# DeltaNet mixer: triangular inversion over all four TensorE quarters, with the second direction half a level behind

## What is computed

```python
a_mat = jnp.where(strict, jnp.einsum('bhnik,bhnjk->bhnij', kb, k) * decay, 0.0)
rhs = jnp.concatenate([v * beta[..., None], kb * jnp.exp(gc)[..., None]], axis=-1)
sol = lax.linalg.triangular_solve(a_mat + jnp.eye(CHUNK, dtype=jnp.float32), rhs,
                                  left_side=True, lower=True, unit_diagonal=True)
```

```python
m = jnp.einsum('nd,de->ne', cond, w_ada_l.astype(jnp.float32)) + b_ada_l.astype(jnp.float32)
```

## Time and profile before

| | |
|---|---|
| median of 3 runs | 2075.03 us (2072.61 to 2078.57) |
| profiled execution, its own time | 2079.55 us |
| its span, first to last instruction | 2077.8 us |
| granted TensorE clock, mean | 0.929 |
| PE, PEld busy | 85%, 70% of the span |
| DVE, ACT, POOL busy | 62%, 46%, 10% |
| T, XX, YY products in the span | 5120 records on line 1100, with x0 |

### The profile page before, as it was taken

One profiled execution on the slowest core, in us unless ns is written; L12 is line 12 of the kernel. 1 busy time (PEld: TensorE's weight loads), 2 busy tenths in 40 slices (PEclk: granted clock), 3 DMA queues, 4 the chain that ended last, 5 costly groups with the idle time before them and its releaser, 6 DMA issues. The chain is left out here.

```text
span 2077.8 us, 40338 instructions
## 1 busy us (share of the span) xinstructions
PE 1763.5 (85%) x15365; PEld 1455.0 (70%) x15366; DVE 1296.8 (62%) x1885; ACT 961.8 (46%) x1490; POOL 209.0 (10%) x267
## 2 busy tenths in 40 slices
PE   3998879899696799999919988899986939999992
PEld 0898678788454588888818986788873527888882
DVE  2388255556445696896663883556662368999674
ACT  2244523233312786786432454333332138888651
POOL 0000022222000100000020001212220010000001
PEclk7999999999797899999959999999997969999996
DMA  7221093420313798897643111331004059999854
GB/s 313 71 82 44 31 358 126 154 102 2 107 59 152 285 384 340 335 401 286 228 153 98 55 44 51 127 125 52 3 2 145 31 209 385 397 398 397 355 199 165
DMA packets 112110, 376.64 MB, mean 181 GB/s; under 512 B 14730, under 2 KB 35490, under 8 KB 86374
## 3 DMA queue, kind: packets, MB, share of 16 engines
q1 hardware_dynamic: 83310, 303.85, 39.2%
q10 hardware_dynamic: 20168, 39.89, 5.0%
q0 software_dynamic: 8496, 30.94, 4.0%
HBM read 332.87 MB, written 41.78 MB: 180 GB/s over the span
## 5 line engine op out<-in xcount | busy, mean ns | idle before, releaser
L1955 DVE TENSOR_TENSOR expert_w_lo<-shared,expert_w_hi 128x2048 fp32r<-128x2048 f32 x192 | 430.6, 2285 | 44.6 <-ACT expert_w_hi L1897 44.3
L1897 ACT ACTIVATE expert_w_hi<-shared 128x2048 fp32r<-128x2048 f32 x192 | 360.6, 1915 | 42.4 <-PEq L141 37.8
L1839 PE MATMUL ps<-expert_w_hi,expert_x_hi 128*128 128x512 f32 x592 | 232.3, 392 | 5.1 <-DVE expert_x_lo L1951 5.1
L1840 PE MATMUL ps<-expert_w_lo,expert_x_hi 128*128 128x512 f32 x592 | 232.0, 392 | 0.0
L1841 PE MATMUL ps<-expert_w_hi,expert_x_lo 128*128 128x512 f32 x592 | 232.0, 392 | 0.0
L1839 PEld LDWEIGHTS ps<-expert_w_hi,expert_x_hi 128*128 128x128 f32 x592 | 112.2, 190 | 29.3 <-issue 5.9
L1841 PEld LDWEIGHTS ps<-expert_w_hi,expert_x_lo 128*128 128x128 f32 x592 | 112.1, 189 | 23.5
L1840 PEld LDWEIGHTS ps<-expert_w_lo,expert_x_hi 128*128 128x128 f32 x592 | 112.1, 189 | 23.2
L1875 PE MATMUL ps<-expert_w_hi,expert_hid_hi 128*128 128x512 f32 x296 | 118.5, 400 | 2.2 <-ACT expert_hid_hi L1929 1.2
L1011 POOL TENSOR_TENSOR mixer_NTb<-mixer_Bt,consts_sb 128x256 f32<-128x256 f32 x120 | 88.4, 760 | 286.3 <-DVE mixer_Bt L1286 222.7
L1876 PE MATMUL ps<-expert_w_lo,expert_hid_hi 128*128 128x512 f32 x296 | 115.4, 390 | 0.0
(11 more groups left out here) (344 smaller groups left out, 3741.1 us busy)
## 6 DMA issues: line engine op xcount, KB each, us to landing
shared<-in_w_gate SPq DMA_DIRECT2D x64, 1024.0 KB, 7.1
shared<-in_w_up SPq DMA_DIRECT2D x64, 1024.0 KB, 8.7
shared<-in_w_down SPq DMA_DIRECT2D x64, 1024.0 KB, 9.0
qkv<-in_w_ada SPq DMA_DIRECT2D x20, 1280.0 KB, 6.0
shared<-in_w_in SPq DMA_DIRECT2D x10, 2048.0 KB, 7.8
y_table<-expert_y ACTq DMA_DIRECT2D x37, 512.0 KB, 8.8
qkvT<-in_w_ada SPq DMA_DIRECT2D x20, 768.0 KB, 8.4
y_table<-zero ACTq DMA_DIRECT2D x1, 12800.0 KB, 50.9
```

What stands on the lines that cost most here:

```text
L1839: pe.matmul(bank, hi, w_hi[:, j, w], start=first, stop=False)
L1840: pe.matmul(bank, hi, w_lo[:, j, w], start=False, stop=False)
L1897: act.activation(w_hi[:, j, :], raw[:, j, :], ACT.Copy).then_inc(w_hi_done, 1)
L1955: dve.tensor_tensor(w_lo[:, j, :], raw[:, j, :], w_hi[:, j, :].bitcast(F32), ALU.subtract).then_inc(w_lo_done, 1)
```

## The change

Direction 1 keeps Y and T1 in the other half of the partitions (`place`), so that its T and XX products use the upper right and lower left quarters of the array, while direction 0 keeps the diagonal ones. Direction 1 lags by half a level: TensorE interleaves T of direction 0 with XX of direction 1 of the level before, product by product, then makes YY of direction 1; then it interleaves XX of direction 0 with T of direction 1, then makes YY of direction 0. YY stays in the diagonal quarters in both directions. `turn(n0)` and `next_scores(n0 + 1)` now stand between these two halves of level 2 and of level 3. x0 of both directions is interleaved too and waits for both Y. VectorE's first Y is written in two halves, since the halves change place. The order of the other instructions on VectorE, ScalarE, GpSimd and SyncE is as it was; the modulation units are as they were.

```diff
+        def place(d, b):
+
+            return b if d == 0 else 1 - b
...
-                def eight(b, c, lhsT, rhs, sem):
-
-                    for h in range(DH):
-                        for r in range(2):
-                            mm = pe.matmul(G.ps[half(r), b, 256 * c + h * HB:256 * c + (h + 1) * HB],
-                                           lhsT(h)[half(r)], rhs(h)[half(r)], start=True, stop=True)
-                    mm.then_inc(s_[sem], 1)
+                def x0(d, h, b):
+                    y = half(place(d, b))
+                    return pe.matmul(G.ps[half(b), d, h * HB:(h + 1) * HB], Y[y, d, h, :], G.c("eye")[y], start=True, stop=True)
+
+                def t1(v, d, h, b):
+                    return pe.matmul(G.ps[half(place(d, b)), d, h * HB:(h + 1) * HB], NTb[half(b), v % 2, d, h, :], X[half(b), d, h, :],
+                                     start=True, stop=True)
+
+                def xx(d, h, b):
+                    y = half(place(d, b))
+                    return pe.matmul(G.ps[half(b), d, 256 + h * HB:256 + (h + 1) * HB], Y[y, d, h, :], T1[y, d, h, :],
+                                     start=True, stop=True)
+
+                def yy(d, h, b):
+                    y = half(place(d, b))
+                    return pe.matmul(G.ps[y, 2 + d, h * HB:(h + 1) * HB], T1[y, d, h, :], Y[y, d, h, :], start=True, stop=True)
+
+                def wait_t1(s, v, d):
+                    pe.wait_ge(s_["nt_done"], lev(s, v, d))
+                    if v == 0:
+                        pe.wait_ge(s_["x0_done"], at(s, d))
+                    else:
+                        pe.wait_ge(s_["x_done"], lev(s, v - 1, d))
+
+                def wait_xx(s, v, d):
+                    pe.wait_ge(s_["t1_done"], lev(s, v, d))
+                    if v:
+                        pe.wait_ge(s_["y_done"], lev(s, v - 1, d, LV - 1))
+                    else:
+                        pe.wait_ge(s_["qk_done"], at(s, d))
+
+                places = [(h, b) for h in range(DH) for b in range(2)]
...
-                    for d in range(2):
-                        pe.wait_ge(s_["y0_done"], at(s, d))
-                        eight(d, 0, lambda h: Y[:, d, h, :], lambda h: G.c("eye"), "x0_p")
-                    for v in range(LV):
-                        for d in range(2):
...
-                            eight(d, 0, lambda h: NTb[:, v % 2, d, h, :], lambda h: X[:, d, h, :], "t1_p")
+                    pe.wait_ge(s_["y0_done"], at(s, 1))
+                    for h, b in places:
+                        m0 = x0(0, h, b)
+                        m1 = x0(1, h, b)
+                    m0.then_inc(s_["x0_p"], 1)
+                    m1.then_inc(s_["x0_p"], 1)
+                    for v in range(LV + 1):
+                        if v == 0:
+                            wait_t1(s, v, 0)
+                            for h, b in places:
+                                m0 = t1(v, 0, h, b)
+                            m0.then_inc(s_["t1_p"], 1)
+                        elif v < LV:
+                            wait_t1(s, v, 0)
+                            wait_xx(s, v - 1, 1)
+                            for h, b in places:
+                                m0 = t1(v, 0, h, b)
+                                m1 = xx(1, h, b)
+                            m0.then_inc(s_["t1_p"], 1)
+                            m1.then_inc(s_["xx_p"], 1)
+                        else:
+                            wait_xx(s, v - 1, 1)
+                            for h, b in places:
+                                m1 = xx(1, h, b)
+                            m1.then_inc(s_["xx_p"], 1)
+                        if v:
+                            for h, b in places:
+                                m1 = yy(1, h, b)
+                            m1.then_inc(s_["yy_p"], 1)
                         if v == 2:
                             turn(n0)
                         if v == 3:
                             next_scores(n0 + 1)
-                        for d in range(2):
-                            pe.wait_ge(s_["t1_done"], lev(s, v, d))
...
-                            eight(d, 1, lambda h: Y[:, d, h, :], lambda h: T1[:, d, h, :], "xx_p")
-                            eight(2 + d, 0, lambda h: T1[:, d, h, :], lambda h: Y[:, d, h, :], "yy_p")
+                        if v < LV:
+                            wait_xx(s, v, 0)
+                            wait_t1(s, v, 1)
+                            for h, b in places:
+                                m0 = xx(0, h, b)
+                                m1 = t1(v, 1, h, b)
+                            m0.then_inc(s_["xx_p"], 1)
+                            m1.then_inc(s_["t1_p"], 1)
+                            for h, b in places:
+                                m0 = yy(0, h, b)
+                            m0.then_inc(s_["yy_p"], 1)
...
-                        dve.tensor_tensor(Y[:, d], NTb[:, 1, d], row(G.c("eye"), DH), ALU.add).then_inc(s_["y0_done"], 1)
+                        for b in range(2):
+                            ins = dve.tensor_tensor(Y[half(place(d, b)), d], NTb[half(b), 1, d], row(G.c("eye")[half(b)], DH), ALU.add)
+                        ins.then_inc(s_["y0_done"], 1)
...
-                                    ins = dve.tensor_tensor(YF[half(b), d, :, half(b)], Y[half(b), d], blocks(2 + d)[half(b)],
-                                                            ALU.subtract)
+                                    y = half(place(d, b))
+                                    ins = dve.tensor_tensor(YF[half(b), d, :, half(b)], Y[y, d], blocks(2 + d)[y], ALU.subtract)
```

## The result

The changed kernel takes 2081.34 us (median of 20 runs, 2076.69 to 2085.85) against 2075.57 of the kernel before beside it: a ratio of 1.0027, interval 1.0016 to 1.0037. It is slower by 5.8 us where I had forecast 20 us less; the sign was wrong, by a difference of the size that I had called too small to tell.

What follows compares the result with a forecast made beforehand. Bounds per block: TensorE in levels 0 to 3, the division at level 2, VectorE at the end. Order net of Y0 14.5 plus clock 5.3 gave 19.8 us off 2079.55 profiled, so a 2055 us median; range 2047 to 2069.

Steps and rivals of the forecast that it cites:

- order and quarters: Mixer blocks: the new product order and shared quarters were to gain 15.9 us, before Y0's cost of 1.4.
- Y0: VectorE's first Y in four half adds instead of two: 1.4 us more, paid in each layer's first block, elsewhere hidden.
- Four quarters: TensorE: T of one direction and XX of the other run together, a pair taking 0.47 us instead of 0.93.
- quarters take turns: Rival: quarters in one row half take turns, a pair costs 0.93 us, kernel slower at 2093 us; chance 0.11.
- Division alone: Softmax division at level 2 runs without GpSimd's work beside it; `turn` 7.94 us after first T, not 9.62: 1.68 gained.
- division keeps its neighbour: Rival: GpSimd's masks still run beside the division, the gap stays long, only 4.3 us gained, 2071; chance 0.08.
- Levels 0 and 1: Levels before the division: next pair 0.05 us after X; both levels faster, yet only 0.11 us reaches the division.
- After the turn: From `turn` to the value products: 2.19 us instead of 2.95, so 0.76 gained per block.
- The end: Level 4, bound by VectorE: T1L, which ends the block's inversion, comes later, 0.27 us lost per block.
- Faster work would meet those stalls sooner: nothing: First block of layer 0, with TensorE queue stalls of 2 to 3 us: its gain was put at nothing.
- Clock: TensorE's shorter gap before `turn` restores granted clock behind it in five slow stretches: 5.3 of 8.8 us returned.
- the clock stays low: Rival: granted clock stays low after the shorter gap, leaving only 14.5 us gained, 2061 to 2067 us; chance 0.25.

Runs made afterwards that it cites:

- after_noload_fill: Changed kernel without unit loads after the first, plus two idle TensorE products ahead of `turn`; 1964.93 us, 0.9467 of the kernel before.
- before_noload_fill: Kernel before without unit loads after the first, plus two idle TensorE products ahead of `turn`; 1965.20 us, ratio 0.9468.
- second pair: Both kernels run again with the same code for a second trace each: kernel before 2072.97 us (one run), changed kernel 2077.11 us.
- after_again: The changed kernel once more, same code, for a second trace; 2077.11 us, 1.0015 of the kernel before.
- after_hoist: Changed kernel with waits on masks, Y and a pair's first products moved ahead of the preceding YY group; 2078.29 us, 1.0021 of the kernel before.
- after_late: Changed kernel with the load of level 3's unit held, from the second block, until both directions' YY of level 1; 2081.09 us, ratio 1.0026.
- fill kernels: Kernels with two idle TensorE products added ahead of `turn`; with unit loads and no other edit: kernel before 0.9975, changed kernel 0.9961.
- before_late_fill: Kernel before with the load of level 3's unit delayed and two idle TensorE products ahead of `turn`; 2063.05 us, 0.9946 of the kernel before.

## Why the prediction was wrong, step by step

| step | forecast, us | shown | by |
|---|---|---|---|
| order and quarters | -15.9 | -7.0 | after_noload_fill less before_noload_fill, blocks behind the first |
| Y0 | +1.4 | +3.7 | first x0 of each layer, full clock |
| clock and stalls | -5.3 | +5.0, second pair +7.7 | rest of the ten inversions' sums: 249.4 - 251.6 + 7.2, 246.7 - 246.2 + 7.2 |
| sum | -19.8 | +1.5, second pair +4.2 | inversions (-2.2, +0.5) and Y0; timed: +5.8 (3.3 to 7.7), again 1.0015 |

7.2 is the order's worth in all ten inversions of the filled kernels without loads, 238.9 less 231.7. Near as the sums come to the timed difference, the traces don't show that difference itself. From its first product to its last instruction the mixer takes, both layers together, 572.1 and 569.0 us in the two traces of before and 570.5 and 569.1 in those of the changed kernel: level. Low clock ahead of the first x0 costs before 1.63 in both layers of both traces, after in one layer and after_again in none, which hides about half of Y0 in the first pair and nearly all of it in the second; the rest of the balance lies between the inversions. (The spans of the second pair differ by 3.5 us, all of it outside the mixer, in code that the change leaves alone.) So what took the forecast gain away is located, and why the changed kernel is then slower by 0.15 to 0.27%, and not level, stays open.

**Four quarters: right.** A pair costs 0.51, not 0.93. The rule of the Trainium skill ("TensorE: Matmul & The Clock Gate", Part 3, The mechanism), that a weight load overlaps matmuls only in another row group, is not borne out by this trace: two quarters of each pair share a row half, their records start 0.01 us apart, and the 32 take 0.51. The rival "quarters take turns" falls.

**Division alone: right.** From Y (460.79) to `turn` (462.65) 1.86, forecast 0.34 + 0.20 + 1.14 + 0.14 + 0.06 = 1.88. The rival "division keeps its neighbour" falls.

**Levels 0 and 1: the term was mis-sized.** I took 0.05 from the end of X to the next pair, the hand-over of a group with its waits spread out. Measured are 0.19 to 0.34. The pair has four waits; with two, 0.16 (after_hoist): so part of the gap is the waits, shown, and the rest I don't know. Y of b comes at 6.77 (460.79 - 454.02) instead of 6.42 (6.20 and 0.22 for 512 keys), so `turn` is 0.33 late.

**After the turn: the same term.** 3.32 and 3.54 at full clock, forecast 3.75 and 3.97 less 0.76: 0.33 short. **The end: the same term again.** T1L comes 0.51 later than in the earlier trace rows, not 0.27. Together 0.9 a block, 8.1 over nine: nearly all of the 8.9 that the order fell short. This 0.05 is the step that failed in the order's own sum.

**Y0: wrong place and size.** I put it at 1.4 and paid it in layer 1 alone, since I took the first block of layer 0 as lost to its stalls. It is paid in both, at the full 0.85 for half the partitions, near the upper of my two bounds.

**"Faster work would meet those stalls sooner: nothing": the step that took the rest.** A term was put at nothing. I read the stalls of the earlier trace rows as belonging to the first block and to TensorE's queue as such, and wrote that SyncE's loads stay as they were. They are the ends of program pieces waiting for their packet behind a load's bytes. The changed order passes them at another moment of the same loads and has less work in hand ahead of each, and the traces have 17.8 and 15.7 us of them instead of 12.8 and 10.1. Behind the first block of layer 0 they are 10.4 and 8.6 instead of 5.3 and 3.4. That the loads cause them is shown (the kernels without loads have none there); that a denser order has to meet more of them is only argued: after_late took two away and moved a third, and its time stayed.

**Clock: the direction in the stretch was right, the whole was not.** The five stretches gave back 3.9 of 8.8 (forecast 5.3): two of five full, and those three that stayed low are the blocks with a stall in the levels. In two of them the lower level begins at the stall's end or within it (335.1; 1362.5, stall from 1360.9 to 1363.7), in the third 1.8 us behind it (400.0). This the rival "the clock stays low" hadn't foreseen either: it gave 2061 to 2067. Inside the inversions the low clock grew from 27.3 to 43.9 us. The fill kernels show what that is worth: more in the changed order (0.5 to 0.7%) than in the old one (0.25%).

Open: why one packet of instructions slips in ahead of a load (before, 326 to 328) and another waits 4.5 us; which of the first block's stalls the large zero write beside it makes (not tried); and where the timed loss of 0.15 to 0.27% lies.

## What to carry to other kernels

A faster order on an engine is worth what is left of it after every wait at its new joints: take the hand-over from a row with as many waits as the new place has, not from the shortest one. Before a sum is made, look where an engine's "issue" stalls lie in its count of instructions and which transfers run there; here moving some loads and filling a gap, in the old order, gave 11 us, and the reordering with its waits and Y0 repaired, without the unit loads and with the gap filled on both sides, 6. When a wait is moved forward, check at its new place that it is long met: one mask wait ahead of x0 ate what after_hoist had gained. When edits repair a disturbance that depends on phase, measure them together, since their gains didn't add.

## What was not expected of the hardware

TensorE's program comes in packets of 16 KB (1.69 MB in 103), and all 104 long "issue" stalls of the mixers, behind the start of each phase, stand where a stretch of 256 records ends; with the unit loads of 2 MB running they last 1.0 to 3.7 us outside the first block of layer 0, and without those loads only that first block has any. The Trainium skill ("Runtime: NRT & Kernel Launch", Instruction fetch mechanics) has the piece and the 256 instructions, and says that crossing into a new one is mostly hidden. Beside bulk loads the runs disagree: 10 to 18 us of such stalls in 2080, and 0.31% back when the loads of before move.

A VectorE add of 64 partitions by 256 columns takes 0.845, one of 128 partitions 0.831: half the partitions save nothing.

Two idle products, 2 us of TensorE work ahead of a `turn` that had to wait anyway, brought the stretch behind it, granted 0.54 to 0.71 in the earlier trace rows, to 1.00 in all five blocks of before_late_fill.
